# One transpose job per direction in 64-row groups, and planes that change places by chunk: a chunked RWKV scan in one Trainium2 core

## The reference

```python
def rwkv_prepare(h, mu, w_in, w0, w1, w2, a0, a1, a2, k_k, k_a):
    ...
    a = heads(jax.nn.sigmoid(a0[:, None, None, :] + ...))
    kk = (kkf / jnp.maximum(jnp.linalg.norm(kkf, axis=-1, keepdims=True), 1e-12)).astype(h.dtype)
    k_dir = k[None] * (1.0 + (a - 1.0) * k_a.reshape(RWKV_HEADS, RWKV_HEAD))
    b = kk[None] * a
    return r, logw, k_dir, v, -kk, b, gate

def wkv_scan(r, logw, k, v, a, b, s0):
    ...
    def step(s, inp):
        r_t, lw_t, k_t, v_t, a_t, b_t = inp
        sa = jnp.einsum('dbhij,dbhj->dbhi', s, a_t)
        s = s * jnp.exp(lw_t)[..., None, :] + sa[..., None] * b_t[..., None, :] + v_t[..., None] * k_t[..., None, :]
        return s, jnp.einsum('dbhij,dbhj->dbhi', s, r_t)
    ...

def rwkv_readout(y, prep, r_k, lnx_g, lnx_b, w_out):
    ...
    yf = y[0] + jnp.flip(y[1], 1)
    ...
    o = (yn + bonus.reshape(B, T, D)) * jax.nn.silu(gate)
    return o @ w_out
```

## Time and profile before

| | |
|---|---|
| median of 3 runs | 2210.26 us (2209.57 to 2217.8) |
| the profiled execution | 2212.54 us |
| its span | 2210.9 us |
| the scan stage within the span | about 1200 to 1890 us |
| TensorE busy, whole span | 2027.3 us (92%) |
| VectorE busy, whole span | 1010.4 us (46%) |
| ScalarE busy, whole span | 538.8 us (24%) |

### The profile page before, as it was taken

How to read it: one execution, slowest core, us unless ns; L and a number is a source line. 1 busy time by engine, 2 the same in 40 slices (tenths; PEclk the granted TensorE clock), 3 DMA queues, 4 the chain that set the end, 5 groups by cost and what they waited for, 6 DMA issues and landing times. The chain is left out here.

```text
span 2210.9 us, 40677 instructions
## 1 busy us (share of the span) xinstructions
PE 2027.3 (92%) x17304; PEld 1496.0 (68%) x17304; DVE 1010.4 (46%) x2284; ACT 538.8 (24%) x989; POOL 289.9 (13%) x525
## 2 busy tenths in 40 slices
PE   4998999899999998999998888999999888879998
PEld 3887888778888885888883445555555554346656
DVE  5551552553341165388608445545553541242273
ACT  1112121332000102300112533534434431011162
POOL 0000000000000000000000643434443130000100
PEclk8999999999999999999999998999999899989999
DMA  8554336445884430487415865556565362103200
GB/s 370 201 210 162 115 153 214 96 167 218 329 330 160 155 139 35 193 321 307 187 39 230 257 175 127 154 145 174 163 169 147 67 228 90 77 6 114 76 1 20
DMA packets 127841, 360.25 MB, mean 163 GB/s; under 512 B 78896, under 2 KB 87600, under 8 KB 110256
## 3 DMA queue, kind: packets, MB, share of 16 engines
q1 hardware_dynamic: 94480, 210.31, 27.5%
q0 software_dynamic: 32608, 146.31, 19.3%
q10 hardware_dynamic: 576, 1.05, 0.1%
HBM read 340.76 MB, written 16.85 MB: 162 GB/s over the span
## 5 line engine op out<-in xcount | busy, mean ns | idle before, releaser
L306 PE MATMUL bank<-h,ring 128*128 128x256 f32 x2112 | 459.4, 381 | 0.3 <-PEq L146 0.3
L306 PEld LDWEIGHTS bank<-h,ring 128*128 128x128 f32 x2112 | 402.9, 191 | 57.5 <-issue 2.3
L2249 PE MATMUL bank<-rw_feed 128*128 128x512 f32 x464 | 244.5, 639 | 14.3 <-ACT rkv L2436 7.7
L2008 POOL DMA_DIRECT2D rw_feed<-rwkv_mixes x232 | 124.8, 538 | 539.0 <-PE bank L2249 380.9
L1055 PE MATMUL bank<-ffn_hidden,ring 128*128 128x256 f32 x704 | 152.9, 379 | 3.4 <-PEq L1225 3.4
L1055 PEld LDWEIGHTS bank<-ffn_hidden,ring 128*128 128x128 f32 x704 | 133.6, 190 | 22.2 <-issue 4.1
L527 PE MATMUL bank<-h,ring 128*128 128x256 f32 x640 | 143.1, 380 | 1.1 <-PEq L323 1.1
L2543 DVE TENSOR_TENSOR rw_u<-bank,rw_lam 128x128 f32<-128x128 f32 x120 | 34.1, 284 | 227.0 <-PE bank L2159 223.0
L527 PEld LDWEIGHTS bank<-h,ring 128*128 128x128 f32 x640 | 120.2, 190 | 20.2 <-issue 4.8
L2249 PEld LDWEIGHTS bank<-rw_feed 128*128 128x128 f32 x464 | 78.2, 195 | 74.4 <-issue 42.6
L2009 POOL DMA_DIRECT2D rw_feed<-in_rkvg x232 | 124.6, 537 | 10.0 <-issue 10.0
(11 more groups left out here) (440 smaller groups left out, 3192.2 us busy)
## 6 DMA issues: line engine op xcount, KB each, us to landing
ring<-in_stream SPq DMA_DIRECT2D x79, 2048.0 KB, 8.5
rw_feed<-rwkv_mixes POOLq DMA_DIRECT2D x232, 256.0 KB, 3.1
next_w<-in_mod_stream POOLq DMA_DIRECT2D x24, 2048.0 KB, 10.7
ctx<-in_mod_rest POOLq DMA_DIRECT2D x16, 1024.0 KB, 7.3
rw_feed<-in_rkvg POOLq DMA_DIRECT2D x232, 64.0 KB, 3.5
y<-bias_table SPq DMA_DIRECT2D x48, 128.0 KB, 5.0
rwkv_mixes<-ring SPq DMA_DIRECT2D x6, 1024.0 KB, 4.2
rw_at<-rw_at_kept SPq DMA_DIRECT2D x16, 256.0 KB, 5.1
```

Of the source, the lines that this page charges most:

```text
L306: mm = pe.matmul(out, ring_tile(k, n, kt, i * P), rhs[kt], start=start and kt == kts[0], stop=stop and kt == kts[-1])
L2008: pool.dma_start(feed[:, g % FEED, 0:512], mixes[j, :, g % KT, :]).then_inc(fed[g % FEED], 16)
L2249: pe.matmul(k.psum[PROJ], feed[:, g % FEED, 512:], feed[:, g % FEED, 0:512], start=(kt == 0), stop=(kt == KT - 1)).then_inc(eaten, 1)
```

## The change

The diff, cut to its core. `krows` and `brows` were functions of h alone; `plane` wrote a kind at one place in all chunks.

```diff
-        out += [("atok", n, d, half) for half in range(2)]
+        out += [("atok", n, d)]
         out += [("akv", n, d, e) for e in range(2)]
-        out += [("pq", n, d, e, half) for half in range(2) for e in range(2)]
+        out += [("pq", n, d, e, odd) for odd in range(2) for e in range(2)]
...
-    shape = {"lora": 1, "akv": 2, "pq": 2, "gr": 3, "gram": 4}
+    shape = {"lora": 1, "atok": 1, "btok": 1, "akv": 2, "pq": 2, "gr": 3, "gram": 4}
...
+            x = buf[:, 0, kind, :]
+            return bass.AP(x.tensor, x.offset, [list(x.ap[0]), [512 + LCH * (1 - 2 * kind), 2], [2 * LCH, 8], [1, LCH]])
...
-        def krows(h):
-            return slice(64 * h, 64 * h + 32)
+        def krows(h, c2):
+            at = 64 * h + 32 * (c2 // 4)
+            return slice(at, at + 32)
+        def brows(h, c2):
+            return krows(h, 7 - c2)
...
-                        sp.dma_start(blocks(at_dram, n, d, h), BG[n % 3][d][brows(h), :, :, 96:128].rearrange(
-                            "p c e t -> p (c e) t")).then_inc(at_out, 16)
+                        for half in range(2):
+                            sp.dma_start(blocks(at_dram, n, d, h, half), in_place(n, d, h, half)).then_inc(at_out, 16)
...
-                        sp.dma_start(BG[n % 3][d][brows(h), :, :, 96:128].rearrange("p c e t -> p (c e) t"),
-                                     blocks(mt_dram, n, d, h)).then_inc(mt_in, 16)
+                        for half in range(2):
+                            sp.dma_start(in_place(n, d, h, half), blocks(mt_dram, n, d, h, half)).then_inc(mt_in, 16)
...
-            def turned(out, src):
-                for j in range(4):
-                    mm = pe.transpose(out[:, j * P:(j + 1) * P], src(j), ident)
+            def turned(outs, src):
+                for j in range(8):
+                    for e in range(2):
+                        mm = pe.transpose(outs[e][:, 64 * j:64 * j + 64], src[rows64(e), 2 * j:2 * j + 2].rearrange(
+                            "p c k s -> p (c k s)"), ident[rows64(e), rows64(e)])
...
-                for c in range(NCK):
-                    h, c2 = c % 2, c // 2
-                    mm = pe.matmul(out[brows(h), 64 * c2:64 * c2 + 64], BG[n % 3][d][krows(h), c2, e, 96:128],
-                                   VQ[n % 2][d][krows(h), c2, e, :], start=True, stop=True)
+                for j in range(4):
+                    for c2 in (j, 4 + j):
+                        for h in range(2):
+                            mm = pe.matmul(out[brows(h, c2), 64 * c2:64 * c2 + 64], BG[n % 3][d][krows(h, c2), c2, e, 96:128],
+                                           VQ[n % 2][d][krows(h, c2), c2, e, :], start=True, stop=True)
...
-                pe.wait_ge(pq_down, 4 * u + 2 * half + 2)
+                pe.wait_ge(pq_down, 4 * u + 4)
                 pe.wait_ge(btok_down, 2 * u + 2)
...
-                ins = v.scalar_tensor_tensor(plane(VA[n % 2][d], 1), chunks(kk, d), -1.0, chunks(ee, 0), ALU.mult,
-                                             ALU.mult)
+                for a in range(2):
+                    ins = v.scalar_tensor_tensor(VA[n % 2][d][:, 8 * a:8 * a + 8, 1 - a, :], chunks(kk, d)[:, a], -1.0,
+                                                 chunks(ee, 0)[:, a], ALU.mult, ALU.mult)
```

More of the change, by code:

```diff
@@ L1810, in stage_rwkv_scan @@
         kind, n = item[0], item[1]
-        jobs = {"lora": [(0,), (1,)], "gram": [(0,), (1,)], "gr": [(0,), (1,)], "btok": [()],
-                "atok": [()], "akv": [()], "pq": [()],
+        jobs = {"lora": [(0,), (1,)], "gram": [(0,), (1,)], "gr": [(0,), (1,)], "btok": [(0,), (1,)],
+                "atok": [(0,), (1,)], "akv": [()], "pq": [()],
                 "kk": [()], "bonus": [()] if item[2:] == (0,) else [],
@@ L2083, in key_values, with solved @@
                 mm.then_inc(akv_up, 1)
                 free(akv_down, 2 * u + e + 1, "akv", n, d, e)
-            def solved(n, d, e, half):
+            def solved(n, d, e, odd):
                 u = 2 * n + d
-                pe.wait_ge(mt_in, 64 * (n + 1))
+                pe.wait_ge(mt_in, 128 * (n + 1))
                 pe.wait_ge(akv_down, 2 * u + e + 1)
[L2090 to L2093, removed]
-                              ident[krows(h), krows(h)], VQ[n % 2][d][krows(h), at, e, :], start=True, stop=True)
-                for j in range(4):
-                    c2 = 4 * half + j
-                    for h in range(2):
-                        x, y = VQ[n % 2][d][brows(h), c2, e, :], KP[d][brows(h), c2, e, :]
+                out = take("pq", n, d, e, odd)
+                for half in range(2):
+                    for h in range(2):
+                        rows = krows(h, 4 * half)
+                        pe.matmul(out[rows, 256 * half:256 * half + 256].rearrange("p (c v) -> p c v", c=2)[:, :, 64:128],
+                                  ident[rows, rows], VQ[n % 2][d][rows, 4 * half + odd:4 * half + 4:2, e, :], start=True,
+                                  stop=True)
+                for j in (0, 2, 1, 3):
+                    c2 = 2 * j + odd
+                    for h in range(2):
+                        rows = brows(h, c2)
+                        x, y = VQ[n % 2][d][rows, c2, e, :], KP[d][rows, c2, e, :]
@@ L2099, in solved @@
                         both = bass.AP(x.tensor, x.offset, [list(x.ap[0]), [y.offset - x.offset, 2], [1, 64]])
-                        mm = pe.matmul(out[brows(h), j * P:(j + 1) * P], BG[n % 3][d][brows(h), c2, e, 96:128], both,
-                                       start=True, stop=True)
+                        mm = pe.matmul(out[rows, j * P:(j + 1) * P], BG[n % 3][d][rows, c2, e, 96:128], both, start=True,
+                                       stop=True)
                 mm.then_inc(pq_up, 1)
-                free(pq_down, 4 * u + 2 * half + e + 1, "pq", n, d, e, half)
+                free(pq_down, 4 * u + 2 * odd + e + 1, "pq", n, d, e, odd)
@@ L2380, in _ @@
                         act.wait_ge(spilled, 32)
[L2381 to L2382 removed]
+                    for e in range(2):
+                        nc.scalar.copy(BG[n % 3][d][:, :, e, 0:64], bank(*item, e).rearrange(
+                            "p (c j) -> p c j", c=8)).then_inc(btok_down, 1)
                 elif kind == "atok":
[L2384 to L2386 removed]
+                    d = item[2]
+                    act.wait_ge(atok_up, 2 * n + d + 1)
                     if n >= 2:
                         act.wait_ge(step_up, NSTEP * (n - 1))
[L2389 to L2390 removed]
+                    for e in range(2):
+                        nc.scalar.copy(VQ[n % 2][d][:, :, e, :], bank(*item, e).rearrange(
+                            "p (c j) -> p c j", c=8)).then_inc(atok_down, 1)
                 elif kind == "akv":
```

81 lines of the change are left out of this document (37 added, 44 removed).

## The result

The changed kernel takes 2250.68 us (median of 4, 2241.84 to 2255.05) against 2210.66 for the kernel before on the same chip: ratio 1.016, interval 1.0132 to 1.0188 (the two medians alone give 1.018). The prediction was 2220, range 2196 to 2236. The profiled execution has a span of 2248.5 us, 37.6 more than before. TensorE's matmuls did get cheaper, and it waits more.

A forecast was written before the change was run, and what follows sets the result against it. TensorE's matmuls were taken to pace stages 1 to 4 and 6, VectorE and DMAs stages 0 and 5. New waits less savings summed to +10.1 on 2212.54, 2222.6, less 2.3 for the median: 2220, range 2196 to 2236.

The forecast's parts named there:

- The places of the waits: TensorE waiting at a head's first `pq` for DMAs, second `gram` for VectorE, `gr` and second direction's `akv` for ScalarE.
- the sizes of three: Waits at the second `gram` 1.8, `gr` 1.0 and second direction's `akv` 1.3 us: 4.1 in a middle stage.
- the reciprocal: Second `gram` of a stage: VectorE's reciprocal, 0.95 us, stands ahead of `el`, within a wait of 1.8 us.
- wait 1: First `pq`, for the inverse's DMAs: waits of 2.8, 1.2, 1.7, 1.7 us in stages 1 to 4, 4.5 in stage 6.
- The issues' upper bound of 0.69: SyncE's queue: four more DMA issues take up to 2.8 us instead of 1.6, adding 1.2 a head, 7 in six.
- The savings: TensorE's matmuls per head: turns 1.76, `akv` 1.7, `pq` 2.1 saved, shape changes 0.65 lost, 4.9 us less together.
- the estimate for them is 0.80: Rival, chance 0.05: matmuls start at least about 25 ns apart, 32 `akv` instructions take 0.80 us; total near 2228.
- The clock: Rival, chance 0.13: new gaps ahead of `pq` lower TensorE's clock in one or two stages, 2 to 3 us each; 2226.
- Stages 5 and 6: Stage 5, paced by VectorE: split `el` writes and longer queue, +0.6; stage 6: waits 4.5 + 2.3 less 4.9, +1.9.
- The sum: Whole kernel: each stage's new waits less its savings, with +3.4 for head and stage 0, give +10.1 us.

The follow-up runs named there:

- e8_el_first: Changed kernel with the readout's variance, square root and reciprocal moved behind the second `el` in five stages: 2248.23 us, ratio 1.0149.
- e4_filled_wait: Changed kernel with three 128x512 matmuls on constants ahead of the first `pq`'s DMA wait in heads 1 to 7: 2243.42 us, ratio 1.0138.
- e1_turns_alone: Kernel before with only the new turns and the item order that comes with them, four DMAs each way: 2245.26 us, ratio 1.0139.
- e5_old_places: Changed kernel with its items at the places of before, an empty item replacing each second turn job: 2215.51 us, ratio 1.0009.
- e2_planes_alone: Changed kernel with the old turns and so the order of before, eight DMAs each way: 2208.42 us, ratio 0.9974.
- e6_old_places_filled: `e5_old_places` with two 128x512 matmuls on constants ahead of the first `gram` of stages 0 to 5: 2208.46 us, ratio 0.9978.

## Why the prediction was wrong

- **The places of the waits** were right, all four, and so were the sizes of three: 1.8, 1.0 and 1.3 forecast, 1.32, 0.72 and 1.17 measured, 3.2 a stage instead of 4.1. `e8_el_first` shows that the reason given for the first of them (the reciprocal) was only 0.4 us of it.
- **The step that failed first** is wait 1, "the last landed about 3.05 after its own issue began" and "four more issues are 1.6 at 0.4". I took one landing, from stage 0, for all stages. In stages 1 and 2 the landing came 14.9 and 15.0 us after the stage's start, where the prediction had 12.6 for stage 1 (1433.9 less 1421.28). Of the 2.3 us between them in stage 1, 1.45 are the landing behind the issuing (4.02 instead of 2.57), 0.6 the issuing (eight issues took 4.12, forecast 3.5), 0.2 its later start. TensorE's arrival was right there: 10.0 us after the start (1440.99 - 4.85 - 1426.10), forecast 9.8. So the waits of stages 1 to 4 and 6 are 19.7 us together where I had 11.9. The waits of stages 3 and 6 came within 0.6 of the forecast. The issues' upper bound of 0.69 was in the text, but the landing behind the last issue got no upper bound, and it took 1.6 to 4.25 over the stages. And that an issue costs less for half of the bytes was wrong: it took 0.47 to 0.69 as before.
- **The savings** were mis-sized: 4.9 us a head forecast, 3.75 in the balance of stage 3. `akv` gave 1.36 for 1.7, `pq` 1.35 for 2.1, the turns 1.04 for 1.76. The two row groups of a turn do run side by side (a turn took 0.64 to 0.79 with its shape change, one after the other 0.88), and so do four of `akv`. 32 `akv` instructions take 0.58 with the shape change behind them. The Trainium skill ("TensorE: Matmul & The Clock Gate", Part 1, "Wait — 56ns, not 53.3ns?") has matmuls start at least about 25 ns apart, by which the estimate for them is 0.80; the trace does not agree. I priced the jobs by their columns and took one shape change for each pair of kinds.
- **The clock** is the largest term that the sum put at nothing. It was a rival of 0.13 with "one or two stages, 2 to 3 us each". It fell behind the first `pq` in each of stages 1 to 4 and 6, 2.9 us lost in stage 1 and about 1.7 in each of the others, and over the whole execution up to 16 us more were withheld than before. The price was right and the count wrong. `e4_filled_wait` takes 13 of the 16 away and is 7 us faster.
- **Stages 5 and 6.** I gave +0.6 and +1.9, and they grew by 6.6 and 6.5. In stage 5 the second `gram` waits 2.37 and `akv` 0.94 and 1.17, all new; in stage 6 `gr` waits 4.00 instead of 1.44 for the `pq` copies, which I had not looked for on ScalarE's queue: I followed who waits for the copy, but not what stands ahead of it.
- **The sum.** Stage 2 by its terms: waits +7.0 (3.49, 1.32, 0.72, 1.17, and 0.48 at the bonus, less 0.15 at the first `gram`), clock +1.7, work -3.8: +4.9, as measured. Forecast: +0.4. Over the whole scan the gap between +10 forecast and +37.6 measured is, as an estimate, 8 of DMA waits, 8 or 9 of savings that did not come (by stage 3), up to 16 of the clock, less 4 or 5 for the three waits that were shorter than forecast.

The cause is shown by the moves: with the places of before the changed kernel is at 2215.5, with one item a head moved at 2220.4. `e1_turns_alone` shows that the order costs as much with four DMAs, through other waits and the clock, so no single wait is the cause. What stays open is why the mean clock of `e5_old_places` is lower than that of `e2_planes_alone` (0.9615 and 0.9645 in the median of ten), from which it differs in the turns alone; its longer wait at the first `gram` was not tested apart from its turns. Why the fill costs the kernel before as much as 9 us is shown only in part: at the first `gram` of its stage 1 there is no wait to fill, and the stage takes 77.7 us with the fill instead of 76.2. In single profiled executions the clock's falls in stages 4 to 6 lie at different places in each kernel, and no run separates them.

## What to carry to other kernels

When the order of a program comes from a list's length or a sort by kind, changing how many items a job has moves jobs that were not touched: compare the order first, and pin the places (an empty item was enough) before judging the edit. A consumer that now stands earlier does not gain time, it waits for the same landing; take the landing from the slowest stage; and follow on each queue what stands ahead of the awaited copy. A job that waits can be the cover of the next wait on the same engine: moving it away uncovers that one. Ask what the clock does behind each new wait, in every stage where it stands, and look at the granted clock of all runs before explaining a difference of a few us.

## What the runs showed of the hardware

- TensorE can pay for a wait twice: after 3.49 us idle the granted clock was 0.72 and 0.85 over 8 us (1.7 us lost), and after a wait of 1.89 us 0.71 and 0.94 over 20 us (3.5 us lost). Not always: the waits of 1.82 and 1.83 in stages 2 and 3 of before left it at 1.00 (1421 to 1657). With matmuls on constants in the waits at the first `pq` it stayed at 1.00 (`e4_filled_wait`), and with them at the first `gram` the times of ten executions lay within 7 us instead of 15 (`e6_old_places_filled`, `e5_old_places`).
- Four row groups of 32x32 tiles run abreast: 32 `akv` instructions took 0.58 to 0.66 us with the shape change behind them; with two groups a job alone took 1.01.
- Splitting DMAs of 64 KB into two of 32 KB made the issuing of eight take 3.8 to 5.5 us, 0.47 to 0.69 each, as each of the four before: an issue costs the same at half the size. The last of eight landed 1.6 to 4.25 us after the issuing.
